# The order of the query tiles in an attention loop, in a two-block layer kernel on one Trainium2 core

## The reference, cut to what matters

```
for each query block of 128, head h, and branch in (selected, window):
    s = (q * scale) @ k.T - slope[h] * (t - kpos)      # masked to kpos <= t
    p = softmax(s)
    o = p @ v
o = g0 * o_cmp + g1 * o_selected + g2 * o_window
```

## Time and profile before

| what | value |
|---|---|
| median of 3 runs | 1701.74 us |
| the profiled execution's own time | 1701.64 us |
| its span | 1699.8 us |
| PE busy | 1663.9 us, 98% of the span |
| DVE busy | 733.6 us, 43% |
| ACT busy | 645.0 us, 38% |
| POOL busy | 649.7 us, 38% |
| mean granted TensorE clock | 0.995 of 2.4 GHz |

### The profile page before, as it was taken

How to read it: one execution, slowest core, us unless ns; L and a number is a source line. 1 busy time by engine, 2 the same in 40 slices (tenths; PEclk the granted TensorE clock), 3 DMA queues, 4 the chain that set the end, 5 groups by cost and what they waited for, 6 DMA issues and landing times.

```text
span 1699.8 us, 22370 instructions
## 1 busy us (share of the span) xinstructions
PE 1663.9 (98%) x7892; PEld 1346.8 (79%) x7892; DVE 733.6 (43%) x1168; ACT 645.0 (38%) x963; POOL 649.7 (38%) x276
## 2 busy tenths in 40 slices
PE   7999999999999999999999999999999999999997
PEld 6888888888887668888888888878877788887885
DVE  5333330215437755333332033678769631653322
ACT  5233321333335663332232123573544532434432
POOL 3444444443341013444444444443323224444444
PEclk9999999999999999999999999999999999999999
DMA  4222232334221002232223223222111112332232
GB/s 167 101 95 99 99 98 87 99 114 146 83 79 50 2 1 87 87 99 98 90 96 99 97 88 112 87 87 75 62 62 63 64 59 99 112 102 90 92 99 87
DMA packets 41955, 149.26 MB, mean 88 GB/s; under 512 B 4784, under 2 KB 4912, under 8 KB 41648
## 3 DMA queue, kind: packets, MB, share of 16 engines
q1 hardware_dynamic: 40112, 142.36, 25.1%
q10 hardware_dynamic: 1792, 6.19, 1.1%
HBM read 145.39 MB, written 2.10 MB: 87 GB/s over the span
## 4 chain that ended last, share of the span: by engine, by line
PE 62%; issue 24%; POOL 7%; DVE 6%; ACT 1%; DVEq 0%; DMA 0%; POOLq 0%; SPq 0%; ACTq 0%
PE ps L508 14%; PE ps L510 14%; PE ps L509 14%; POOL w_lo L469 6%; PE ps L592 2%; PE ps L591 2%; PE ps L590 2%; PE ps L745 1%; PE ps L759 1%; PE ps L769 1%; DVE scr L2014 1%; PE ps L1008 1%; PE ps L1098 1%; PE ps L1096 1%; PE ps L1097 1%
## 5 line engine op out<-in xcount | busy, mean ns | idle before, releaser
L469 POOL TENSOR_TENSOR w_lo<-w_raw,w_hi 128x1024 fp32r<-128x1024 f32 x262 | 636.6, 2430 | 939.2 <-ACT w_hi L1132 930.9
L1132 ACT ACTIVATE w_hi<-w_raw 128x1024 fp32r<-128x1024 f32 x260 | 275.6, 1060 | 892.7 <-PE ps L510 651.6
L508 PE MATMUL ps<-h_hi,w_hi 128*128 128x512 f32 x1048 | 410.7, 392 | 1.6 <-POOL w_lo L469 0.6
L509 PE MATMUL ps<-h_lo,w_hi 128*128 128x512 f32 x1048 | 408.2, 389 | 0.0
L510 PE MATMUL ps<-h_hi,w_lo 128*128 128x512 f32 x1048 | 407.9, 389 | 0.0
L508 PEld LDWEIGHTS ps<-h_hi,w_hi 128*128 128x128 f32 x1048 | 196.7, 188 | 46.1 <-issue 2.5
L510 PEld LDWEIGHTS ps<-h_hi,w_lo 128*128 128x128 f32 x1048 | 196.7, 188 | 41.5
L509 PEld LDWEIGHTS ps<-h_lo,w_hi 128*128 128x128 f32 x1048 | 196.8, 188 | 40.2
L508 PE MATMUL ps<-n_hi,w_hi 128*128 128x512 f32 x512 | 206.3, 403 | 0.7 <-POOL w_lo L469 0.7
L510 PE MATMUL ps<-n_hi,w_lo 128*128 128x512 f32 x512 | 202.7, 396 | 0.0
L509 PE MATMUL ps<-n_lo,w_hi 128*128 128x512 f32 x512 | 202.2, 395 | 0.0
(11 more groups left out here) (317 smaller groups left out, 1863.0 us busy)
## 6 DMA issues: line engine op xcount, KB each, us to landing
w_raw<-in_units SPq DMA_DIRECT2D x262, 512.0 KB, 3.3
x<-in_x SPq DMA_DIRECT2D x4, 512.0 KB, 6.0
w<-in_w ACTq DMA_DIRECT2D x1, 2048.0 KB, 8.1
out<-scr SPq DMA_DIRECT2D x8, 256.0 KB, 2.0
scr<-proj ACTq DMA_DIRECT2D x8, 128.0 KB, 3.1
inv_count<-in_inv_count ACTq DMA_DIRECT2D x1, 1024.0 KB, 5.0
const<-in_const SPq DMA_DIRECT2D x1, 770.0 KB, 9.7
q_sc<-in_row_const ACTq DMA_DIRECT2D x1, 512.0 KB, 3.5
```

Source lines behind the costliest of these rows:

```text
L469: nc.gpsimd.tensor_tensor(w_lo[:, slot, :], w_raw[:, slot, :], w_hi[:, slot, :].bitcast(F32), ALU.subtract).then_inc(w_lo_done, 1)
L508: nc.tensor.matmul(ps[:, bank, :], whi, hi[:, k, :], start=(n == 0), stop=False)
L509: nc.tensor.matmul(ps[:, bank, :], whi, lo[:, k, :], start=False, stop=False)
L1132: nc.scalar.activation(w_hi[:, slot, :], w_raw[:, slot, :], ACT.Copy).then_inc(w_hi_done, 1)
```

## The change

The list of entries takes the query tiles in another order within each (j, b), and the start flag of the value products is set on the first key tile alone:

```
-        PAIRS = [(j, b, qt) for j in range(HPG) for b in range(2) for qt in range(TT)]
+        PAIRS = [(j, b, qt) for j in range(HPG) for b in range(2) for qt in (3, 0, 2, 1)]
```

```
                                                   prob_t[:, 2 * (m % 2) + g, kt * P:(kt + 1) * P],
-                                                  start=(m % PER_J == 0), stop=False, skip_group_check=True)
+                                                  start=(m % PER_J == 0 and kt == 0), stop=False, skip_group_check=True)
```

## The result

The kernel after takes 1709.9 us (median of 11 runs, 1702.04 to 1712.24), the kernel before, beside it on the same chip, 1703.31 us (11 runs, 1700.66 to 1705.46). The ratio is 1.0034 with an interval from 1.0024 to 1.0043: slower by 5.8 us by the ratio (6.6 by the medians), and outside the range given, which ended at 1707.8. The profiled execution took 1709.9 us with a span of 1708.0 us, 8.2 us more than the span before.

What follows compares the result with a forecast made beforehand. PE, busy 98% of the span, bounds the kernel; only idle time and clock are at stake. Waits grow from 7.15 us plus 0.2 to 10.0, 2.7 more, so 1701.64 becomes 1704.3 us; range 1699.8 to 1707.8.

Steps and rivals of the forecast that it cites:

- slot 19: Loop slot 19: a wait of 0.7 us, of which 0.4 us from value products delayed in slot 17.
- slots 5 and 17: New PE waits: 0.4 us in slot 5 behind ACT's copy, 0.7 us in slot 17 at the hand-over of j.
- the tight place: PE's transposes wait for ACT to empty a bank; moves from slots 4k+2 to 4k+3, 4.0 us before, 3.1 after.
- the better neighbour: In the tight slots the widest scores stand beside narrower PE work: a gain of only 0.12 us a block.
- the root's term: Slot 27: PE idles 4.0 us while ACT reaches the square root and reloads its table, 1.35 more than before.
- The flag: Start flag of the value products: changes no count or shape of products, so no time.
- the root's stretch: Low clock behind the square root's wait: stays about as it is, costing 3.1 us.
- the rival in which it falls more often: Two or three of slots 5 to 7, 11, 17 to 19, 23 lower the clock: 1706.0 to 1707.7 us, chance 0.25.
- The rival without the first fall: Same loop waits, but no low clock except behind the root: 1702.6 us, chance 0.25.
- the faster one: DVE ends the tight waits, bias hidden, first clock fall gone: about 1699.0 us, chance 0.10.
- the term that kept the clock's cost as it was: In the loop the first clock fall stays at one, 1.7 us, and the low clock behind the root at 3.1 us.
- the rule weighed in the prediction: Clock drops only after an idle array: the loop would stay at 2.4 GHz everywhere but behind the root.

Runs made afterwards that it cites:

- after_again: The kernel after, unchanged, run and traced once more: 1710.0 us, ratio 1.0044 to the kernel before.
- flag_alone: The kernel before in its old order, with only the start flag limited to the first key tile: 1703.08 us, ratio 0.9999.
- last_j_old: New order for the first three head pairs, old order for the last: 1705.17 us, ratio 1.0009 to the kernel before.
- only_last_j_new: Old order for the first three head pairs, new order for the last alone: 1707.01 us, ratio 1.0012 to the kernel before.
- pad: Old order with two spreads repeated in slot 31, 2.2 us of added PE work: 1706.74 us, ratio 1.0017 to the kernel before.
- old_pad12: Old order with 12 dummy products in slot 31, 3.3 us of added PE work: 1708.77 us, ratio 1.0033 to the kernel before.
- new_filled: New order with dummy products inside its three longest waits (slots 11, 23, 27): 1705.09 us, ratio 1.0004 to the kernel before.
- new_root_early: New order with ACT's square root moved ahead of the exponent of slot 28: 1706.62 us, ratio 1.0007 to the kernel before.
- wide pair: Old and new order, each with 512-column products added at three sparse places outside the loop: ratios 1.0069 and 1.0114 to the kernel before.
- dense pair: Old and new order, each with 128-column products added at three sparse places outside the loop: ratios 1.0140 and 1.0158 to the kernel before.
- The two halves of the order: last_j_old and only_last_j_new, each with the new order in one part of the head pairs: ratios 1.0009 and 1.0012 to the kernel before.
- the smaller pads: Old order with two repeated spreads, or with 4 dummy products, in slot 31: ratios 1.0017 and 1.0015 to the kernel before.
- new_pad2: New order with 2 dummy products (0.55 us) added in slot 31: 1709.1 us, ratio 1.0036 to the kernel before.
- old_dense: Old order with 128-column products added at three sparse places outside the loop: 1727.84 us, ratio 1.0140 to the kernel before.

## Why the prediction was wrong

*The waits* were right in sum, 10.35 us against 10.0, in their growth, 3.0 against 2.7, and in most places. That the sum is so close is in part luck, since two errors cancel: slot 19 (0.12 for 0.7, and 0.27 in after_again) and slots 5 and 17 (1.85 for 1.1). The worked example of the tight place has a slip: 3.82 - 2.43 - 0.49 is 0.9 us and not 1.0; nothing else was built on it. The tight place moved as described, the better neighbour brought nothing, and the root's term, the largest, was right to 0.1 us. The flag was rightly nothing.

*The clock in the loop* was right in the profiled runs: one fall ahead of slot 18, now at V4 of slot 17, and the root's stretch as long as before. after_again had the first one in slot 23. So the rival in which it falls more often named places where it can fall, but in neither trace did it fall at more than one of them besides the root. The rival without the first fall was wrong too, and so was the faster one.

*The step that failed* stands in the first paragraph: "Outside it PE runs weight units back to back, so what the loop gains or loses moves the end by as much." It does not. PE's work outside has places where little is in the array (L708, L935, the idle 1.84 us ahead of L1079), and the clock may fall there or not. In the two traces of the new order 10.2 us of low clock lie outside the loop, in the two of the old order none: up to 5.1 us. (Of after_again's, 6.8 us lie ahead of the loop, where the order can't have caused them.) No term and no rival of mine had a place outside the loop, which is why the range ended at 1707.8. With it failed the term that kept the clock's cost as it was: over all executions the low clock costs 3.8 us more.

*All executions, not only the profiled ones.* The mean granted clock of each execution is known to 0.001. Its span times (1 - clock) is the time that the low clock can cost at most, and the rest of the span moves with waits and work. The end, low in every trace, is counted too, but cancels between kernels; the rounding is 0.85 us at most in one execution. Means, as differences from the old order (the kernel before in every set of rounds whose clocks are known, and flag_alone: 132 executions), an estimate:

| kernel | executions | span, us | by the clock | the rest |
|---|---|---|---|---|
| after and after_again | 16 | +5.7 | +3.8 | +1.9 |
| last_j_old | 12 | +1.2 | +0.2 | +1.1 |
| only_last_j_new | 12 | +2.4 | +0.5 | +1.9 |
| pad | 11 | +2.4 | +0.6 | +1.9 |
| old_pad12 | 5 | +5.2 | +2.3 | +3.0 |
| new_filled | 12 | +1.1 | -1.8 | +2.9 |
| new_root_early | 12 | +2.1 | +1.6 | +0.5 |

The standard error of the first row's 3.8 is 0.7 us and that of its 1.9 is 0.2. Of the 16 executions of the new order 13 have a mean clock of 0.992 or less, of the 132 of the old order none. The clock's errors in the other rows are 0.3 to 0.9 us. In the wide pair, new over old, the rest makes 3.5 us (error 0.7) and the clock 4.1 with an error of 3.2, in the dense pair 2.6 (0.5) and 1.1 (1.3): too few executions to tell anything of the clock.

*What is shown, and what isn't.* Shown: the flag costs nothing; about two thirds of the new order's loss is granted clock, low in 13 of its 16 executions as in none of the old order's, and the rest, 1.9 us and more, is of the size of the added waits (the low time in which PE waits anyway is counted to the clock). Shown too: filling the waits, or moving the root, takes the loss back to 1.0004 and 1.0007. Not shown: where in the span the low clock of the other executions lies, and why the new order has more of it. That it comes from displacement alone has for it old_pad12, whose clock costs 2.3 us more with no new wait, and, weakly, the smaller pads; against it stands, weakly too, new_pad2, whose trace escapes the low stretches while its median doesn't fall, and the fall near 1130 us that goes with the one at 465. The two halves of the order cost 0.7 us of clock together, the whole 3.8: the clock's part does not seem to add up from parts, as a wait's does. That the longer waits themselves make low stretches in the loop likelier fits new_filled, but its fills also took away the two stretches that the old order has. This stays open.

The clock near 1130 us bears on the rule weighed in the prediction. The fall came with 0.7 us of idle time and, in old_dense at 464 us, with none at all. The Trainium skill, page "TensorE: Matmul & The Clock Gate", section "Part 1: The HAM clock gate", describes the drop as what follows an idle array; by that rule none of these falls should be there. The measurement decides: a stretch in which PE is busy by the trace with narrow products can lose the clock as well.

## What to carry to other kernels

Work out waits slot by slot from pace and chain: it gave the sum of the waits to 0.35 us here, with single terms off by up to 0.6. But before writing that a local change moves the end by as much, read the granted clock of the whole span for sparse places downstream, and widen the range by what each of them would cost if the clock fell there (1.7 to 3.4 us each here). Look at the mean clock of every execution beside its time: it divides a difference between clock and waits, which one trace can't. Where a wait can't be removed, work that keeps PE busy in it, or a table load moved ahead of the chain, can be worth more than the wait's own length.

## What the runs showed of the hardware

- The start's low clock lasted longer in some executions than in others, in kernels identical up to there: the same product of L508 starts at 17.89 us in one trace and at 19.95 in another, 2.1 us by chance.
- In ten of 16 traces the clock fell at 465 us among 64 products of 31 columns that are the same in all, and the group took 5.5 to 5.9 us where it takes 4.39.
- The same instructions at the same distance from each other kept the clock at 1124.76 and lost it at 1128.60 (1.00 and 0.77 over the 15 us behind).
- Sixteen added products of 128 columns among those of 31 columns turned a low stretch of at most 6.8 us into one of 27.3 us, with PE busy for all of it; with 15 more products at two other places the kernel became 24 us slower for an estimated 8.5 us of products. Eight products of 512 columns at the same place left 17.1 us.
- Span less half of the low time and less the shift at the start nearly reproduces the spans: (1708.0 - 1699.8) - (20.4 - 10.2) / 2 - (19.22 - 17.90) = 1.8 us for the first pair of traces and (1709.1 - 1701.1) - 5.1 - (19.73 - 19.30) = 2.5 us for after_again against flag_alone. That is near the 1.9 us that all executions give without the clock, and below the 3.0 us of added waits.
